# Low parts of whole weight pieces: an accumulating DMA in place of GpSimd's subtraction

## What is computed

```python
for l in range(DEPTH):
    h = layer_norm(a * h + 0.5 * swiglu(h, ffn1_w_gate[l], ffn1_w_up[l], ffn1_w_down[l]), ln1_g[l], ln1_b[l])
    z = h @ w_in[l]
    ...
    y_pool = pool_mixer(u_pool, w_pool[l], pool_scale[l])
    y_gla = gla_mixer(q, k, v, r, g_lr, w_gate_up[l], b_gate[l], gla_norm_g[l])
    y = jnp.concatenate([y_pool, y_gla], axis=-1) @ w_out[l]
    h = layer_norm(a * h + y, ln2_g[l], ln2_b[l])
    h = layer_norm(a * h + 0.5 * swiglu(h, ffn2_w_gate[l], ffn2_w_up[l], ffn2_w_down[l]), ln3_g[l], ln3_b[l])
return h[:, N_META:]
```

## Time and profile before

| | |
|---|---|
| time, median of 3 runs | 1950.2 us (1948.57 to 1951.83) |
| span of the profiled execution | 1948.2 us |
| busy: PE, DVE, ACT, POOL | 1877.5, 1232.9, 825.3, 446.8 us |
| granted TensorE clock, mean over the span | 0.973 |
| DMA from SP's queue | 171.78 MB |

### The profile page before, as it was taken

How to read it: one execution, slowest core, us unless ns; L and a number is a source line. 1 busy time by engine, 2 the same in 40 slices (tenths; PEclk the granted TensorE clock), 3 DMA queues, 4 the chain that set the end, 5 groups by cost and what they waited for, 6 DMA issues and landing times.

```text
span 1948.2 us, 34609 instructions
## 1 busy us (share of the span) xinstructions
PE 1877.5 (96%) x14406; PEld 1795.0 (92%) x14406; DVE 1232.9 (63%) x1834; ACT 825.3 (42%) x1297; POOL 446.8 (23%) x200
## 2 busy tenths in 40 slices
PE   8999999999899999999999999999898999999996
PEld 8999999988899999999999999999897778899895
DVE  5728547667448837728487385576674488286475
ACT  4525435452125434525455254354521255345353
POOL 4030211432222240030521303023322221402113
PEclk9999999999898999999999999998998989999998
DMA  4233323321111332233322333233211113333232
GB/s 152 98 93 107 115 77 109 108 66 55 44 55 44 106 101 98 90 96 109 119 76 98 98 108 107 91 100 97 66 55 52 46 55 101 105 109 109 87 113 83
DMA packets 48828, 175.26 MB, mean 90 GB/s; under 512 B 5408, under 2 KB 5408, under 8 KB 48672
## 3 DMA queue, kind: packets, MB, share of 16 engines
q1 hardware_dynamic: 48240, 171.78, 26.9%
q10 hardware_dynamic: 432, 1.25, 0.2%
HBM read 170.92 MB, written 2.10 MB: 89 GB/s over the span
## 4 chain that ended last, share of the span: by engine, by line
PE 85%; DVE 10%; ACT 2%; issue 2%; DMA 1%; POOL 0%; DVEq 0%; ACTq 0%
PE PS L371 13%; PE PS L372 13%; PE PS L373 13%; PE PS L424 12%; PE PS L427 12%; PE PS L426 12%; PE PS L381 2%; PE PS L403 2%; PE PS L382 2%; DVE qt L1499 1%; PE PS L712 1%; PE PS L524 1%; DVE h_lo L1145 1%; PE PS L679 1%; DVE ex L1483 1%
## 5 line engine op out<-in xcount | busy, mean ns | idle before, releaser
L330 POOL TENSOR_TENSOR w_lo<-raw,w_hi 128x1024 fp32r<-128x1024 f32 x172 | 431.9, 2515 | 1474.2 <-ACT w_hi L862 1061.5
L371 PE MATMUL PS<-h_hi,w_hi 128*128 128x264 f32 (+1 forms) x1238 | 370.2, 299 | 0.7 <-DVE h_lo L1145 0.4
L372 PE MATMUL PS<-h_lo,w_hi 128*128 128x264 f32 (+1 forms) x1238 | 369.7, 299 | 0.0
L373 PE MATMUL PS<-h_hi,w_lo 128*128 128x264 f32 (+1 forms) x1238 | 369.4, 298 | 0.0
L862 ACT ACTIVATE w_hi<-raw 128x1024 fp32r<-128x1024 f32 x240 | 215.1, 930 | 231.5 <-PE PS L373 179.4
L371 PE MATMUL PS<-x_hi,w_hi 128*128 128x264 f32 (+2 forms) x796 | 243.9, 306 | 11.5 <-DVE ft L1537 7.4
L424 PE MATMUL PS<-v_hi,s_hi 128*128 128x264 f32 (+1 forms) x864 | 245.0, 284 | 6.1 <-DVE s_lo L1211 6.1
L426 PE MATMUL PS<-v_lo,s_hi 128*128 128x264 f32 (+1 forms) x864 | 244.3, 283 | 0.0
L427 PE MATMUL PS<-v_hi,s_lo 128*128 128x264 f32 (+1 forms) x864 | 243.9, 282 | 0.0
L371 PEld LDWEIGHTS PS<-h_hi,w_hi 128*128 128x128 f32 x1238 | 233.0, 188 | 9.3 <-DVE h_lo L1145 1.8
L372 PE MATMUL PS<-x_lo,w_hi 128*128 128x264 f32 (+2 forms) x796 | 241.4, 303 | 0.0
(11 more groups left out here) (217 smaller groups left out, 3997.8 us busy)
## 6 DMA issues: line engine op xcount, KB each, us to landing
raw<-in_stream SPq DMA_DIRECT2D x316, 512.0 KB, 3.6
raw_first<-in_stream SPq DMA_DIRECT2D x4, 512.0 KB, 5.7
out_t<-X SPq DMA_DIRECT2D x8, 256.0 KB, 2.1
X<-in_x_t SPq DMA_DIRECT2D x7, 264.0 KB, 7.3
par<-in_params ACTq DMA_DIRECT2D x2, 480.0 KB, 3.6
X<-in_x_t ACTq DMA_DIRECT2D x1, 264.0 KB, 4.5
```

The source lines that it names most:

```text
L330: nc.gpsimd.tensor_tensor(w_lo[:, slot, :], raw[:, slot % RAWS, :], w_hi[:, slot, :].bitcast(F32), ALU.subtract).then_inc(lo_done[slot], 1)
L371: nc.tensor.matmul(o, hi, rhs_hi[:, k, tok], start=first, stop=False)
L372: nc.tensor.matmul(o, hi, rhs_lo[:, k, tok], start=False, stop=False)
L373: return nc.tensor.matmul(o, lo, rhs_hi[:, k, tok], start=False, stop=last)
```

## The change

For whole pieces ACT writes, right after `w_hi`, a second copy of the raw piece with scale -1.0 into `w_lo` (in fp32r, so it is the negated high part). POOL waits for that and issues a DMA that reads the raw piece from HBM once more and adds it to `w_lo`. POOL subtracts no more. SP may reload the raw buffer when ACT's second copy is done.

```diff
+def by_dma(n):
+    return n >= SLOTS and whole(n)
...
         def wait_piece(eng, n):
-            eng.wait_ge(lo_done[n % SLOTS], n // SLOTS + 1)
+            eng.wait_ge((lo_added if by_dma(n) else lo_done)[n % SLOTS], lo_value(n))
...
             for n in range(SLOTS + RAWS, DEPTH * LAYER_PIECES):
-                wait_piece(sp, n - RAWS)
+                if by_dma(n - RAWS):
+                    sp.wait_ge(S["raw_neg"], negated(n - RAWS))
+                else:
+                    wait_piece(sp, n - RAWS)
                 sp.dma_start(raw[:, n % RAWS, :], stream[n // RAWS, n % RAWS]).then_inc(raw_full[n % RAWS], 16)
...
             def split(n):
                 slot = n % SLOTS
-                pool.wait_ge(S["raw_hi"], n + 1)
-                nc.gpsimd.tensor_tensor(w_lo[:, slot, :], raw[:, slot % RAWS, :], w_hi[:, slot, :].bitcast(F32),
-                                        ALU.subtract).then_inc(lo_done[slot], 1)
+                pool.wait_ge(S["raw_neg"], negated(n))
+                pool.dma_start(w_lo[:, slot, :], stream[n // RAWS, n % RAWS],
+                               accum_op=ALU.add).then_inc(lo_added[slot], 16)
...
                 nc.scalar.activation(w_hi[:, n % SLOTS, part], raw[:, n % RAWS, part], ACT.Copy).then_inc(S["raw_hi"], 1)
+                if whole(n):
+                    negative(n)
+            def negative(n):
+                nc.scalar.activation(w_lo[:, n % SLOTS, :], raw[:, n % RAWS, :], ACT.Copy, scale=-1.0)\
+                    .then_inc(S["raw_neg"], 1)
...
                 nc.scalar.activation(w_hi[:, n % SLOTS, :], raw[:, n % RAWS, :], ACT.Copy).then_inc(S["raw_hi"], 1)
+                negative(l * LAYER_PIECES + n)
```

More of the change, by code:

```diff
@@ L117, in whole, with lo_value, negated @@
     return True
+def by_dma(n):
+    return n >= SLOTS and whole(n)
+def lo_value(n):
+    same = [i for i in range(n % SLOTS, n + 1, SLOTS) if by_dma(i) == by_dma(n)]
+    return len(same) * (16 if by_dma(n) else 1)
+def negated(n):
+    return sum(by_dma(i) for i in range(n + 1))
 def stream_ready(l, idx):
@@ L267, in matmul_parts @@
             return [(PS[ps][:, i, 0:n], slice(first + i * n, first + (i + 1) * n)) for i in range(count)]
-        names = """par_loaded consts consts_dve masks raw_hi piece_done out_stored setup row_sync
+        names = """par_loaded consts consts_dve masks raw_hi raw_neg piece_done out_stored setup row_sync
             silu_done prod_done h_hi_done h_lo_done down_evac
@@ L288, in build @@
         lo_done = [sem(f"lo_done{i}") for i in range(SLOTS)]
+        lo_added = [sem(f"lo_added{i}") for i in range(SLOTS)]
         block = ctx.enter_context(nc.Block())
```

## The result

The changed kernel takes 1988.6 us in the median of four runs (1984.5 to 1990.8), the kernel before 1950.3 (1948.6 to 1951.8) on the same chip: the ratio is 1.02, with a 95% interval of 1.0188 to 1.0212. It is slower by 38 us, where 1948 was forecast. The profiled execution spans 1986.8 us.

The account below looks back on a forecast made before the run. PE bounds the feed-forward networks, DVE the mixers and layer norms. -35 + 13.2 (`u_copy`) + 13.2 (piece 4) + 6 (half clock) = -2.6 us from 1948.2, plus 2.0 for the median: 1948; range 1928 to 1985, likeliest 1942 to 1960.

Parts of the forecast that it names:

- The gain: Without POOL's 172 subtractions DVE's stops go: 35 us, of which 27 in two mixers and 6.8 in layer norms.
- D: Time from POOL's wait to the added DMA's landing: estimate 6.8 us, below 3.3, above 10.
- The first down piece of each phase: PE waits there for D - 6.8 = 0 at the estimate; each microsecond beyond costs 12.
- the four places: Piece 4 of each network, where PE waits for the added low part: 13.2 us in all.
- the slow rival: Slow added DMA, late at twelve first down pieces and four pieces 4: 1967 at D = 8; chance 0.25.
- A wait of 1.5 us: Such a wait among full-rate matmuls brings no slow stretch, so no clock loss was added for `u_copy`.
- Piece 4: First piece after those the norm's end uses: PE waits D - 3.5 = 3.3 us, plus 6 us at half clock for four.
- `u_copy`: Last fast pair of each phase: behind two negated copies, PE starts P7 1.1 us late, 12 times, 13.2 us lost.
- Norms after a network: Layer norms following a feed-forward network: `sum_x` no longer held behind POOL, gain 1.0 us each, three of them.
- so I count nothing: At the mixers' head, raw pieces loaded 1.4 us earlier but beside the accumulating DMA: no gain or loss.
- Its chances: Forecast 0.35, quick DMA 0.28, slow DMA 0.25, smaller gain 0.12; faster 0.40, slower 0.42, same 0.18.

Follow-up runs that it names:

- Run 1: The kernel before with POOL's subtraction cut to 8 of 1024 columns, most of each low part left out: 1902.5 us, ratio 0.9764.
- run 8: The changed kernel with SP's next raw load held until the adding DMA of the same raw buffer has landed: 2089 us.
- Run 10: The changed kernel with the DMA copying instead of adding, and SP's next raw load held until it has landed: 1996 us.
- run 6: The changed kernel with POOL subtracting 8 of 1024 columns after ACT's negated copy in place of the adding DMA: 1917.7 us, ratio 0.9838.
- run 3: The changed kernel with the DMA copying the raw piece over `w_lo` instead of adding it: 1924.3 us, ratio 0.988.
- run 5: The changed kernel, but POOL subtracts 16 pieces: piece 4 of each network and the first down piece of each phase. 1926.8 us, ratio 0.9889.
- run 2: The changed kernel with POOL subtracting over ACT's negated copy in place of the DMA, SP waiting for that: 1988.1 us, ratio 1.0197.

## Why the prediction was wrong

**The gain was right.** The stops of DVE, the mixers' waits and the half-clock stretches behind them went as read from the profile: 33.6 us measured in mixers and the norms behind them, for 30.8 in the forecast. Run 1 shows that I had under-priced the stops themselves (46 us in all, for 35).

**The step that failed is D, "I take the middle ... Estimate D = 6.8 us".** It came out at 7.8 in the median and 9.2 at the phase end shown above. Its parts were the right ones and two were too small. Adding was to cost 1.6 us for reading the destination, and costs 1.7 alone (5.7 against 4.0, runs 8 and 10), so the size was right; that it is the reading, no run shows. The base was the plain load's 3.6, but the copy from POOL's queue takes 4.0; it also writes fp32r where SP's load writes float32, and no run parts the two. The load beside it was to cost 1.6, and costs 2.1 when the DMA adds. The sum 3.6 + 1.6 + 1.6 becomes 4.0 + 1.7 + 2.1.

The Trainium skill ("DMA: Bandwidth & Descriptors", section "Anatomy of one DMA — SWDGE (gpsimd) path") gives an estimate of 3.2 us by its fit. Run 10's trace has 3.6 at best and 4.0 in the median for the copy, so the fit is low here even without adding. The Trainium skill ("DMA: Bandwidth & Descriptors", section "Issuing engines are not separate DMA queues") says that DMAs issued by different engines run on the same 16 DMA engines and interleave. The traces agree: 7.8 us beside the load, 5.7 without.

**"The first down piece of each phase ... waits for D - 6.8 = 0 at the estimate, but every microsecond beyond costs 12."** The budget was right: 6.6 us were to spare at 348.94. The value of D there was not, nor that one value stood for all. The twelve first down pieces landed 6.2 to 9.2 us after POOL's start, five of them after 8.9 or more. PE waited 19.8 us for eleven of them, and 4.0 us more at six later down pieces, all in third phases, where a piece is short. What makes some landings slower than others at the same place is open. The slowest are the second down pieces, which start 1.9 us behind the first (9.7 us in the median), and PE waits for none of them.

The wrong D does not carry the whole miss. With 7.8 in the prediction's own sum the four places cost 17.2 in place of 13.2, the twelve 12 in place of 0, and the time is 1964. Even the slow rival, which named this mechanism and place, has 1967 at D = 8, and the chip 1988.6. Of the 25 us that are left, some 12 are the scatter of D (23.8 us of waits at down pieces, for 12), some 8 are stretches at half clock, and 5 are the norms after a network.

**Clock.** "A wait of 1.5 us ... is followed by no slow stretch" held for `u_copy`. But the waits at the down pieces grew longer than that. Behind four of them, of 2.5 to 3.4 us, the granted clock fell to 0.50 for 3.4 us (from 351.6, 713.4, 846.6 and 1699.9), 6.3 us lost in all; behind one of 2.4 us at 1100.2 it did not fall. At the network starts the stretches cost 8.1 us for four, where I had 6.

**Piece 4.** D - 3.5 gives 4.3 at the median D. PE waited 15.7 us in four places, 2.9 to 4.5 each, with D from 6.3 to 7.9 there; the form was right, the value came from D.

**`u_copy`.** The place was right, twelve times, and the size nearly. PE stands idle for 0.7 to 0.8 us, 8.6 in all, and by the starts P7 comes 0.95 to 1.1 us later than before, 11.8 in all for the forecast's 13.2: the copies take 0.95 us each in a row. (In the trace of the kernel before, `u_copy` signals 0.40 us after its start, not 0.35.)

**Norms after a network.** I forecast a gain of 1.0 each, and they lost 2.1 us together. What `sum_x` gains came, 3.3 us. I had not looked at the ACT instructions ahead of the last `sq`: a raw piece that comes late, and two copies in front of it. The added DMA, by the raw piece that it delays, has the larger part, 7.5 us in three norms against under 1 for the copies (run 6). The sentence "so I count nothing" on raw pieces beside the added DMA was wrong here: their landing went from 3.6 to 4.3 us in the median, and ACT's waits at its line 973 are 25 us, where they were 2.6 (line 946 before).

**Two sums in the prediction are slightly off.** Its chances give 0.44 for slower (0.25 + 0.12 + a fifth of 0.35), not 0.42, and D = 9 gives 1983, not 1985. Neither touches the forecast.

**What the runs prove, and what they don't.** That D at the tight places is the cause is shown twice: the same DMA with a quicker landing gives 1924 (run 3), and the same DMA with 16 pieces taken out gives 1927 (run 5; 11 of these 62 us are `u_copy`'s). ACT's copies account for 15 us (run 6). Left open is why run 2's later subtraction costs 24 us more than the one in the kernel before. By the stages 12 us of it lie in the phases and 12 in the norms, none in the mixers; what DVE is held up in there, I didn't take further.

## What to carry to other kernels

A transfer in place of an engine's work trades busy time for latency. List for each piece how long its reader can spare, and price the new way at the places with the least to spare, in the company that it has there, not by its median. Then use it only where there is room: the same change pays 2.1% on 60 of the 172 pieces and costs 2% on all of them.

A control that swaps one part (run 2) can hit the same total by another way; a second one that removes that way (run 6) is needed before the number is read.

## What the hardware showed that I had not expected

- The packets of an adding DMA of 512 KB from GpSimd's queue take 2.85 us of all sixteen DMA engines, those of a plain one 1.6 from SP's queue and 1.5 from GpSimd's (13.1% of run 3's 1922 us over 172 pieces). With the load held they take longer, 3.1 and 1.8 (runs 8 and 10), though the DMA lands earlier. In the window 39.5 to 44.4, with two additions and two loads under way, the DMA share is 1.04 and 257 GB/s are moved.
- POOL's own part in such a DMA is 0.86 us. The first packet begins 1.6 us after that instruction starts with the load held, and 2.7 us after it beside the load (medians of run 8 and of the changed kernel).
- The issue from POOL's queue does not stop DVE: no `qt` of 14 takes over 0.706 us, and DVE is busy for 1128.1 us in all, as in run 1, where POOL hardly subtracts.
